# Projection of a hybrid attention layer: the plain quarters kept as high and low parts, low parts on VectorE, the 512-column group first

## What is computed

```python
mod = jax.nn.silu(c) @ w_ada + b_ada
shift, scale, gate = jnp.split(mod, 3, axis=-1)
h = _rmsnorm(x, g_pre) * (1.0 + scale[:, None, :]) + shift[:, None, :]
proj = h @ w_in
(ml_qk, ml_v, ml_o, ml_z, ml_gates,
 sb_q, sb_k, sb_v, sb_z) = jnp.split(proj, IN_SPLITS, axis=-1)
ml_qk = jax.nn.silu(_causal_conv(ml_qk, conv_w, conv_b))
...
h_ml = jax.nn.sigmoid(ml_o.reshape(hs).astype(jnp.float32)) * h_ml
h_ml = _rmsnorm(h_ml, g_ml_head).reshape(B, S, ML_WIDTH)
h_ml = h_ml.astype(x.dtype) * jax.nn.silu(ml_z)
...
h_sb = h_sb.reshape(B, S, SB_WIDTH).astype(x.dtype) * jax.nn.silu(sb_z)
```

## Time and profile before

| | us |
|---|---|
| median of 3 runs | 3735.97 |
| lowest, highest | 3732.03, 3736.85 |
| the profiled execution, its own time | 3735.73 |
| its span, first to last instruction | 3733.9 |
| TensorE busy in the span | 3524.1 (94%) |
| VectorE, ScalarE, GpSimd busy | 2657.4, 2031.6, 801.0 |
| mean granted TensorE clock, share of full | 0.973 |
| projection, from the span's start to the first instruction of the next stage | 1704.9 |

### The profile page before, as it was taken

How to read it: one execution, slowest core, us unless ns; L and a number is a source line. 1 busy time by engine, 2 the same in 40 slices (tenths; PEclk the granted TensorE clock), 3 DMA queues, 4 the chain that set the end, 5 groups by cost and what they waited for, 6 DMA issues and landing times. The chain is left out here.

```text
span 3733.9 us, 68038 instructions
## 1 busy us (share of the span) xinstructions
PE 3524.1 (94%) x24947; PEld 2883.5 (77%) x24947; DVE 2657.4 (71%) x3520; ACT 2031.6 (54%) x4136; POOL 801.0 (21%) x725
## 2 busy tenths in 40 slices
PE   6999949999998999998999999989999999799998
PEld 4888739999998788896777677667777777588887
DVE  4555424456999644677998899889889888466665
ACT  3333213334444433445777777777777777455554
POOL 0333330004334233100011201120001001233332
PEclk8999969999999999998999999999999999899999
DMA  7656646665444777873011101110111001576664
GB/s 266 222 216 230 223 160 216 198 207 194 133 139 135 249 241 246 258 236 128 18 41 53 62 23 36 53 56 22 31 48 51 17 11 32 153 205 199 199 205 136
DMA packets 416198, 517.84 MB, mean 139 GB/s; under 512 B 33104, under 2 KB 327888, under 8 KB 413872
## 3 DMA queue, kind: packets, MB, share of 16 engines
q1 hardware_dynamic: 400176, 459.56, 38.6%
q0 software_dynamic: 15744, 54.54, 4.4%
HBM read 339.74 MB, written 174.26 MB: 138 GB/s over the span
## 5 line engine op out<-in xcount | busy, mean ns | idle before, releaser
L1445 DVE TENSOR_TENSOR_SCAN a_prod<-a_keep,a_prod,a_zeros 128x512 f32<-128x512 f32 x896 | 1076.3, 1268 | 87.8 <-ACT a_keep L1361 84.8
L1370 ACT COPY a_turned<-a_rt 128x512 f32<-128x512 f32 x1088 | 547.1, 588 | 258.5 <-PE a_rt L1315 258.2
L1361 ACT ACTIVATE a_keep<-a_z 128x512 f32<-128x512 f32 (+3 forms) x1152 | 555.5, 573 | 42.1 <-PE a_z L1304 41.9
L1315 PEld LDWEIGHTS a_rt<-a_ident,a_prod 128*128 128x128 f32 x4224 | 453.9, 141 | 134.6 <-issue 62.4
L1315 PE MATMUL a_rt<-a_ident,a_prod 128*128 128x128 f32 x4224 | 533.2, 279 | 25.3 <-DVE a_prod L1445 24.5
L1326 PE MATMUL a_acc<-a_turned,a_dw 128*64 128x256 f32 x4352 | 519.6, 380 | 0.7 <-ACT a_osum L1380 0.7
L708 ACT CAST p_hlo<-p_wraw 128x1024 fp32r<-128x1024 f32 x196 | 205.2, 1047 | 476.4 <-PE p_bank L565 293.2
L928 DVE TENSOR_TENSOR p_hlo<-p_wraw,p_hlo 128x1024 fp32r<-128x1024 f32 x140 | 193.8, 1384 | 368.6 <-ACT p_hlo L708 368.5
L1326 PEld LDWEIGHTS a_acc<-a_turned,a_dw 128*64 128x64 f32 x4352 | 286.5, 136 | 213.2 <-issue 92.0
L1304 PE MATMUL a_z<-a_khi,a_q 64*128 64x512 f32 (+3 forms) x2304 | 373.3, 403 | 1.3 <-DVE a_xe L1431 0.9
L1262 POOL TENSOR_SCALAR_AFFINE_SELECT a_keep<-a_keep 128x256 f32<-128x256 f32 x128 | 66.9, 528 | 1074.3 <-ACT a_keep L1361 1071.4
(11 more groups left out here) (268 smaller groups left out, 5729.5 us busy)
## 6 DMA issues: line engine op xcount, KB each, us to landing
p_wraw<-scratch_sums SPq DMA_DIRECT2D x128, 512.0 KB, 4.5
p_wraw<-scratch_hT SPq DMA_DIRECT2D x96, 512.0 KB, 4.7
p_wraw<-in_x SPq DMA_DIRECT2D x8, 2048.0 KB, 14.9
scratch_hT<-p_hraw SPq DMA_DIRECT2D x8, 2048.0 KB, 7.9
scratch_sums<-p_hraw SPq DMA_DIRECT2D x8, 2048.0 KB, 8.4
p_hraw<-scratch_sbv POOLq DMA_DIRECT2D x32, 512.0 KB, 5.5
m_xt<-in_x SPq DMA_DIRECT2D x32, 512.0 KB, 4.9
out_y<-m_ot SPq DMA_DIRECT2D x32, 512.0 KB, 3.7
```

The costliest lines, as they stand in the source:

```text
L1315: last = pe.transpose(rt[k % RB][:, h * QW + i * P:h * QW + (i + 1) * P], prod[:, u % PB, 2 * i + h, kb * P:(kb + 1) * P], ident[:])
L1361: act.activation(keep[:, at % KB, 0:w], z[at % ZB][:, 0:w], ACT.Sigmoid, scale=-Z_SCALE).then_inc(keep_done, 1)
L1370: act.copy(by_head(turned[:, k % TB]), by_head(rt[k % RB][:])).then_inc(turned_done, 1)
L1445: dve.tensor_tensor_scan(prod[:, u % PB, s, 0:w][:, ::-1], keep[:, at % KB, 0:w][:, ::-1], zeros[:, 0:w], first, ALU.mult, ALU.add).then_i ...
```

## The change

- **Groups.** GATED becomes the direct group: 512 columns, 4 blocks of 24 matmuls with the weights as the stationary side, and the gates as a fifth block. ZV becomes a group of seven products of 24 matmuls of 512 columns. The order is GATED, ZV, SPLIT, CONV, VO.
- **Parts in DRAM.** `scratch_hT` is gone. The three plain quarters of `hhi` and `hlo` go to DRAM as `scratch_parts` (`store_parts`, six stores of 512 KB a chunk), and `load_direct` brings both parts straight to the operand slot, two loads of 512 KB, with no cast and no subtraction. It waits for the product three before.
- **Slots.** The operand has three slots. Sums are loaded four products ahead to one of two raw buffers and made into parts two products ahead. Weight pieces have two buffers in place of three.
- **Low parts.** All are on VectorE. GpSimd makes 32 rounds of weight sums, then `value_steps` without pacing, once the last tile of the convolution is out.
- **Direct stage.** The turns of the next chunk stand behind blocks 1 to 4. The store of the sums stands behind block 0's output. `token_sums` no longer waits for a store. Before block 0 is taken out VectorE runs `root` and `scale_x` of the next chunk, as before.
- **First weights.** Two weight operands and one sum are made on ScalarE ahead of the last chunk's outputs, and SP loads them behind the last `store_parts`.

```diff
-SPLIT, CONV, VO, ZV, GATED = range(5)
+GATED, ZV, SPLIT, CONV, VO = range(5)
 GROUPS = [
-    (ZV, [(C_Z, 512), (C_SV, 512)]),
-    (SPLIT, [(C_SQ, 1024)]),
-    (CONV, [(C_QK, 1024)]),
-    (VO, [(C_V, 1024)]),
-    (GATED, [(C_SZ, 512)]),
+    (GATED, (C_SZ, C_SZ + 256)),
+    (ZV, (C_Z, C_SV)),
+    (SPLIT, (C_SQ, C_SK)),
+    (CONV, (C_QK, C_QK + 512)),
+    (VO, (C_V, C_O)),
 ]
...
+    def direct(self, q):
+        return self.A_OF[q % 7][0] == "a"
...
-    def low_engine(self, q):
-        return "pool" if self.kind(q) == CONV else "dve"
-    def ahead(self, q):
-        return q - 2 if self.kind(q) == GATED else q - 1
...
-        BLOCKS = 9
+        BLOCKS = 5
...
+            def store_parts(m):
+                sp.wait_ge(n_lo, PAIRS * (m + 1))
+                for e, t in enumerate((hhi, hlo)):
+                    src = t[:, m % 2].bitcast(F32)
+                    sp.dma_start(parts_v[m, e, :, 0], src[:, 0:4, 0:HC]).then_inc(hl_out[m % 2], 16)
+                    for th in range(2):
+                        sp.dma_start(parts_v[m, e, :, 1 + th], src[:, 4:8, th * HC:(th + 1) * HC]).then_inc(hl_out[m % 2], 16)
...
+            def load_direct(q):
+                g, n, r = sv.at(q)
+                if q >= 3:
+                    sp.wait_ge(p_done, sv.all_done(q - 3))
...
+                for e in range(2):
+                    sp.dma_start(a_flat[q % 3][e].bitcast(F32), parts_d[n, e][...]).then_inc(ad_in[q % 3], 16)
...
-                    if b == 1:
-                        sp.wait_ge(h_summed, 4 * (n + 1))
-                        sp.dma_start(s_v[n], hraw[:]).then_inc(n_out, 16)
+                    if b == 0:
+                        sp.wait_ge(h_summed, 4 * (n + 1))
+                        sp.dma_start(s_v[n], hraw[:]).then_inc(s_out, 16)
...
+                if step + 2 < NQ and sv.direct(step + 2):
+                    load_direct(step + 2)
+                if 4 <= step + 4 < NQ and not sv.direct(step + 4):
+                    load_sum(step + 4)
+                while next_w < len(PIECES) and sv.w_step(*PIECES[next_w - 2][:2]) <= step:
...
-                    if 3 <= b < 7 and n + 1 < NCH:
-                        turn(n + 1, 2 * b - 6)
-                        turn(n + 1, 2 * b - 5)
+                    if b and n + 1 < NCH:
+                        turn(n + 1, 2 * b - 2)
+                        turn(n + 1, 2 * b - 1)
...
-            def low_a(q):
-                ah, al = a_flat[a_slot(q)]
-                pool.wait_ge(a_hi, q + 1)
-                pool.tensor_tensor(al, flat(araw[q % 3]), ah.bitcast(F32), ALU.subtract).then_inc(a_lop, 1)
...
-                if sv.kinds[g] == VO and r in (1, 4):
...
+            for e in range(NT // 2):
+                value_steps(e)
...
             def high_a(q):
-                act.wait_ge(a_in[q % 3], 16 * (q // 3 + 1))
-                if a_waits(q):
-                    act.wait_ge(p_done, a_waits(q))
+                k = sv.sums_before(q)
+                act.wait_ge(a_in[k % 2], 16 * (k // 2 + 1))
+                if q >= 3:
+                    act.wait_ge(p_done, sv.all_done(q - 3))
...
-            dve.wait_ge(n_out, 32 * m + 16)
...
-                for b in range(4):
-                    evict(b)
-                    if n == 0 and b == 0:
-                        token_sums(0)
+                evict(0)
                 for pair in range(PAIRS):
+                    if pair < 3:
+                        evict(pair + 1)
                     if n + 1 < NCH:
                         spread(n + 1, 2 * pair + 1)
                         low_norm(n + 1, pair)
-                    evict(4 + pair)
...
-                for q in range(step + 1, min(NQ, step + 3)):
-                    if sv.ahead(q) == step and sv.low_engine(q) == "dve":
-                        low_a(q)
+                if step + 2 < NQ and not sv.direct(step + 2):
+                    low_a(step + 2)
```

More of the change, by code:

```diff
@@ L1030, in finish @@
-            def finish(q):
-                g, n, r = sv.at(q)
-                kind = sv.kinds[g]
-                if r < 3 or kind not in (SPLIT, GATED):
-                    return
-                for j in range(sv.banks(q)):
+                        continue
+                    addend = (third if r == 4 else kept)[:, j]
+                    dve.wait_ge(summed, sv.summed(q - r + 2, j))
+                    if kind == CONV:
+                        pair = upair[j + (2 if r != 5 else 0)]
+                        t = slice(3, 3 + HC) if r == 6 else slice(3 + HC, 3 + CH)
+                        if n:
+                            dve.wait_ge(tail_done, 4 * n + (2 if r != 5 else 0) + j + 1)
+                        else:
+                            dve.wait_ge(tail_done, 4)
+                        dve.tensor_tensor(pair[:, :, t], two(addend), two(b[:]), ALU.add).then_inc(summed, 1)
+                    elif (kind == VO and r == 5) or (kind == ZV and r != 5):
+                        dve.wait_ge(st_a[s], 16 * (BASE + USE["a", q, j]))
+                        dve.tensor_tensor(oa[:, s], addend, b[:], ALU.add).then_inc(summed, 1)
+                    else:
+                        dve.wait_ge(*y_free[j])
+                        dve.tensor_tensor(y[:, j], addend, b[:], ALU.add).then_inc(summed, 1)
+                        y_free[j] = (o_hi, HIGH[q, j]) if kind == VO else (o_lo, LOW[q, j])
@@ L1036, in finish @@
+            def finish(q):
+                kind, r = sv.kind(q), q % 7
+                for j in range(2):
                     b, s = bank[ROLE[r] + j], sv.out_slot(q, j)
-                    dve.wait_ge(o_hi, sv.high_at(q, j))
-                    if kind == SPLIT:
+                    if kind == SPLIT and r >= 3:
+                        dve.wait_ge(o_hi, HIGH[q, j])
                         dve.wait_ge(st_b[s], 16 * (1 + USE["b", q, j]))
```

604 lines of the change are left out of this document (256 added, 348 removed).

## The result

| | us |
|---|---|
| before, median of 6 runs beside the changed kernel | 3734.84 |
| changed, median of 6 runs (lowest, highest) | 3708.02 (3706.74, 3720.64) |
| ratio, 95% interval | 0.9942 (0.9923 to 0.9961) |
| span of the changed kernel's profiled execution | 3706.4 |
| projection in it, to the first instruction of the next stage | 1677.31 |

The change gains 27 us by the medians, and 22 (15 to 29) by the ratio, which compares the means of the same runs. The forecast was 51 us. The next stage starts 27.6 us sooner (1677.31, was 1704.91) and the spans differ by 27.5, so in these two executions all of it is in the projection.

The account below looks back on a forecast made before the run. TensorE bounds the projection where nothing goes wrong. Terms: TensorE's work -30, gap -55, first products +3, CONV waits -33, VO waits -11, direct-stage waits +70, value tail +7: -49, rounding the rest to 51 sooner, 3685 us; range 3640 to 3732.

Parts of the forecast that it names:

- The sign: Whole kernel: faster, at a chance of 0.87, against 0.05 for the same and 0.08 for slower.
- Direct stage: Direct stage: a chunk takes 39.5 us, bounds 36 and 43, where it took 50.8; the last chunk begins at 332.
- The two waits per chunk: Direct stage: TensorE waits 3.8 us for scaled x, then again until the spread, done at 25.5 us in a chunk.
- First products: ZV's start: product 0 at 360 us, product 7 at 417; 398 with no wait, at the worst 430.
- ZV's last product: End of ZV: 49 products of 5.43 us after its first seven take 266 us, to 683.
- SPLIT and CONV from 683 to 1334, VO to 1644: Three later groups: SPLIT ends at 1007 us, CONV takes 327 to 1334, VO 304.6 and 5 for waits, to 1644.
- for the turn of the weights: SPLIT's start: 2 us added to the 322 us of its products.
- Direct loads are issued when the product three before ends, 10.9 us ahead: Steady products: direct loads go out 10.9 us ahead, for a landing of 6 to 7 us.
- CONV's gain: CONV: `fir` steps at 0.75 us, VectorE about 37.7 a chunk, under TensorE's 40.3; CONV falls from 360 to 327.
- Value rounds: VO: GpSimd's 16 rounds start some 32 us in, take 18 us each, bounds 17.1 and 20, and end at 1654.
- direct loads come late: Rival, chance 0.08: each of 96 direct loads lands later than 10.9 us after issue; 1 us late gives 3781 us.
- the tail: End of the projection: value rounds end at 1654 us, 7 us behind TensorE.

Follow-up runs that it names:

- e4: The changed kernel with the 2 MB store of the four sums cut into two of 1 MB, the first issued after the third sum: 3695.6 us.
- e2: The changed kernel with the direct loads of SPLIT and CONV issued by GpSimd in place of SP: 3688.6 us.
- e8: The changed kernel with sums stored in halves, SPLIT, CONV and VO direct loads on GpSimd, value rounds cut up in SPLIT, third weight-piece buffer: 3658.8 us, repeat 3660.9.
- e5: The changed kernel with the low parts of the sums' operands in CONV made by GpSimd again, 32 of them: 3710.3 us.
- e10: The kernel of e5 with one more GpSimd subtraction for each direct product in CONV, seven a chunk, results unused: 3727.0 us, ratio 0.9989.
- e3: The changed kernel with GpSimd's 16 value rounds started in SPLIT, once ZV's last outputs are stored, not when the convolution is out: 3711.7 us.
- e1: The changed kernel with a third buffer for weight pieces from the fifth piece on: 3692.6 us.

## Why the prediction was off

The sign, the place and the range held. The forecast, 3685, was 23 us too low: the gain was about half of what it said (27 of 51 by the medians, 22 by the ratio). By its own steps, in the profiled execution:

- **Direct stage: right, a little too long.** The gates' stores are 40.8, 38.4, 36.5, 36.9, 36.5, 36.9 and 34.2 us apart, the first six 37.7 in the mean (39.5 forecast, bounds 36 and 43). The two waits per chunk are the two that it named, for scaled x and for the spread behind the sums' store, and e4 shows the second. The store landed in a median of 7.8 us where the row before had 8.4. By the formula that the prediction quotes from the Trainium skill (DMA: Bandwidth & Descriptors, Anatomy of one DMA) it would be an estimated 6.8: the measured time lies between the two.
- **First products: 348.8 for 360, eighth product 410.6 for 417.** Right in kind: SP's queue behind the pieces.
- **ZV's last product ends where forecast**, SPLIT starts at 679.6 (683).
- **SPLIT and CONV from 683 to 1334, VO to 1644: here it failed.** SPLIT took 12.3 us more than the 324, CONV 9.8 more than the 327, VO 3.8 more than the 310. The failed term is what the sum has for the starts of these groups: 2 us "for the turn of the weights" in SPLIT, 5 in CONV and 5 in VO. I had worked out at ZV's start that a pair of pieces takes 7.7 us for a product of 5.43 and that the direct loads stand behind them on SP, and did not carry that to the other three starts, where it is 7.7 to 8 us for 5.4 or 5.8. In the changed kernel it costs 28.3 us of standing still (9.6 at SPLIT, 10.4 at CONV, 8.3 at VO) and, by the starts of the five products behind the longer waits, 9.0 us of slow matmuls. I forecast 12 for the three. "Direct loads are issued when the product three before ends, 10.9 us ahead" is true of the steady part alone. e2 shows that this is SP's order: with the loads on GpSimd's queue SPLIT and CONV together take 653.4 us, where 651 were forecast and 673.2 came. e8 shows that the ring adds its own part.
- **CONV's gain: the steps right, the reason too narrow.** `fir` at 0.75 and no wait for VectorE in steady CONV are as forecast. VectorE had some 33 us of work a chunk (238.91 in 1050:1340) and not 37.7. I had counted GpSimd's effect on `fir` alone, and some steps behind `fir` had it too (one form of the outputs, L1064, took 1.11 us before and 0.68 now, one of the small copies, L1059, 0.87 and 0.17). e5 and e10 show that it was the amount of GpSimd's work that counted, and that four of seven subtractions would still have been hidden.
- **Value rounds: the pace right, the start wrong.** They took 17.7 us each (18 forecast) and the stage ended 10.7 us behind TensorE (1654 against 1644 forecast). But they started 43.8 us behind VO's start, not 32. The kernel before had 43.9, and the prediction gave no reason for less. VectorE is busy for 40.2 of these 43.8 us; which of its steps sets the start, no run separates. Because TensorE was late as well, the late start costs only some 5 us here: where the rounds were not last, the next stage came 4.0 to 5.8 us behind TensorE (e3, e1).
- **The rival "direct loads come late" had the right place and the wrong form.** Not each of the 96 is late, but those at a change of group, five at over 3 us, with a median landing of 5.2 us and not 11.

So along TensorE -11.2 in the direct stage, +7.8 in ZV, counted from its earlier start, +12.3, +9.8 and +3.8 in the three groups and +0.7 in the tail make the 23 us. The prediction adds its 1654 up along the value rounds. That way the same 23 are 18.8 at VO's start, 11.8 for the rounds' start and -7.3 for the rounds. The direct stage was 11 us shorter than forecast and hid a third of the loss in the groups. That part of the agreement is luck.

## What to carry to other kernels

When a load moves to a queue that waits in order, price it at the places where that queue is behind, not at its steady place: for each change of phase, compare the cycle of the ring ahead of it (landing, cast, subtraction, over the number of buffers) with the pace of the consumer. A buffer taken from one ring to pay for another slot is a cost of its own, and it shows on every engine that serves the ring. And a wait removed early in a stage is worth only what the chain that ends the stage leaves of it: the store in halves moved TensorE's end by 17.5 us and the median by 12.4, with the value rounds last.
